# Second block's convolution: transforms ahead of products, filter layers two rounds apart, low parts on GpSimd

## What is computed

```python
def hyena_filter(length, fw1, fb1, fw2, fb2, fw3, fb3, fw4, freq):
    ...
    h = jnp.sin(freq * (emb @ fw1 + fb1))
    h = jnp.sin(freq * (h @ fw2 + fb2))
    h = jnp.sin(freq * (h @ fw3 + fb3))
    h = (h @ fw4).astype(jnp.float32)
    ...

def long_conv(u, filt):
    length = u.shape[1]
    uf = jnp.fft.rfft(u.astype(jnp.float32), n=2 * length, axis=1)
    kf = jnp.fft.rfft(filt, n=2 * length, axis=0)
    return jnp.fft.irfft(uf * kf[None], n=2 * length, axis=1)[:, :length]

def hyena_operator(u, conv_w, conv_b, filter_params, d_bias):
    uc = short_conv(u, conv_w, conv_b)
    x0, x1, v = jnp.split(uc, 3, axis=-1)
    z = v * x1
    filt = hyena_filter(u.shape[1], *filter_params)
    y = long_conv(z, filt).astype(z.dtype) + z * d_bias
    return y * x0
```

## Time and profile before

| | |
|---|---|
| runs | 3280.17 us median of 3 (3278.62 to 3293.43) |
| profiled execution | 3284.43 us, its span 3282.6 us |
| PE busy | 3092.4 us, 94% of the span |
| DVE, ACT, POOL busy | 50%, 38%, 8% |
| mean granted TensorE clock | 0.97 of full |
| chain that ended last | PE 82%, DVE 9%, ACT 4% |
| `even`, from the last attention rounds to the last inverse | 1780 to 1944 us from the span's start |

### The profile page before, as it was taken

One profiled execution on the slowest core, in us unless ns is written; L12 is line 12 of the kernel. 1 busy time (PEld: TensorE's weight loads), 2 busy tenths in 40 slices (PEclk: granted clock), 3 DMA queues, 4 the chain that ended last, 5 costly groups with the idle time before them and its releaser, 6 DMA issues.

```text
span 3282.6 us, 56668 instructions
## 1 busy us (share of the span) xinstructions
PE 3092.4 (94%) x24038; PEld 2843.1 (87%) x24038; DVE 1642.7 (50%) x2610; ACT 1232.1 (38%) x2089; POOL 255.1 (8%) x315
## 2 busy tenths in 40 slices
PE   6898989999898998999999889999999998999899
PEld 6787979977797997999977678999899998987899
DVE  5655565566555655333384455333443335335655
ACT  4454454434445444222244314212232223235443
POOL 1120010013101000000020110000100001101000
PEclk9999999999998998999999899999999998999999
DMA  4533555653365663333442113333433333343364
GB/s 163 184 119 112 178 194 182 215 169 112 108 198 168 202 228 109 123 103 96 149 133 63 58 57 127 115 121 102 131 117 109 119 115 130 126 149 102 121 195 141
DMA packets 266144, 446.72 MB, mean 136 GB/s; under 512 B 16723, under 2 KB 89316, under 8 KB 265252
## 3 DMA queue, kind: packets, MB, share of 16 engines
q1 hardware_dynamic: 260272, 430.80, 40.7%
q10 hardware_dynamic: 5620, 12.29, 1.1%
HBM read 441.98 MB, written 1.05 MB: 135 GB/s over the span
## 4 chain that ended last, share of the span: by engine, by line
PE 82%; DVE 9%; ACT 4%; issue 2%; DMA 1%; POOL 1%; ACTq 0%; SPq 0%; DVEq 0%; POOLq 0%
PE ps L1101 64%; PE ps L1305 2%; PE ps L1130 2%; DVE split L1815 2%; PE ps L1132 2%; PE ps L1131 2%; DVE AR L1815 2%; PE ps L1242 1%; ACT split L1524 1%; DVE A L1812 1%; DVE A L1867 1%; ACT A L1609 1%; PE ps L1253 1%; PE ps L1228 1%; DVE small L1979 1%
## 5 line engine op out<-in xcount | busy, mean ns | idle before, releaser
L1101 PEld LDWEIGHTS ps<-AR,split 128*128 128x128 f32 x19392 | 2265.0, 189 | 115.0 <-issue 77.5
L1101 PE MATMUL ps<-AR,split 128*128 128x256 f32 x19392 | 2330.7, 281 | 24.7 <-DVE AR L1815 10.6
L1815 DVE TENSOR_TENSOR split<-raw,split 128x1024 fp32r<-128x1024 f32 (+1 forms) x706 | 791.9, 1163 | 860.8 <-ACT split L1524 851.4
L1524 ACT ACTIVATE split<-raw 128x1024 fp32r<-128x1024 f32 (+1 forms) x728 | 682.3, 986 | 812.0 <-PE ps L1101 695.1
L1815 DVE TENSOR_TENSOR AR<-A,AR 128x256 fp32r<-128x256 f32 (+2 forms) x268 | 156.6, 585 | 28.2 <-ACT AR L1583 7.8
L2291 POOL TENSOR_TENSOR A<-A 128x256 f32<-128x256 f32 (+1 forms) x45 | 40.6, 902 | 1646.4 <-ACT A L1532 1483.3
L1812 DVE SCALAR_TENSOR_TENSOR A<-A,ps 128x256 f32<-128x256 f32 (+1 forms) x196 | 96.2, 506 | 125.5 <-ACT A L1567 121.1
L1571 ACT ACTIVATE AR<-A 128x256 fp32r<-128x256 f32 (+1 forms) x132 | 68.4, 525 | 191.6 <-DVE A L1901 191.4
L1567 ACT ACTIVATE A<-ps 128x256 f32<-128x256 f32 (+1 forms) x132 | 63.3, 490 | 151.1 <-PE ps L1101 150.9
L1901 DVE TENSOR_TENSOR A<-ps,A 128x256 f32<-128x256 f32 (+1 forms) x132 | 72.3, 555 | 90.2 <-PE ps L1101 90.0
L1130 PE MATMUL ps<-split,AR 128*128 128x512 f32 (+1 forms) x288 | 113.2, 393 | 0.0
(11 more groups left out here) (235 smaller groups left out, 2235.4 us busy)
## 6 DMA issues: line engine op xcount, KB each, us to landing
mod<-w_mod SPq DMA_DIRECT2D x288, 256.0 KB, 3.9
raw<-w_in SPq DMA_DIRECT2D x120, 512.0 KB, 4.8
raw<-w_gu SPq DMA_DIRECT2D x80, 512.0 KB, 4.7
raw<-ffn_a_in SPq DMA_DIRECT2D x80, 512.0 KB, 4.7
raw<-ffn_b_in SPq DMA_DIRECT2D x80, 512.0 KB, 4.6
raw<-ret_in SPq DMA_DIRECT2D x48, 512.0 KB, 4.6
raw<-w_down SPq DMA_DIRECT2D x44, 512.0 KB, 4.6
raw<-ffn_a_out SPq DMA_DIRECT2D x44, 512.0 KB, 4.7
```

Of the source, the lines that this page charges most:

```text
L1101: mm = e.matmul(out[:, s:s + NT], wt[:, c, m_], xs(k0 + c, a + s, a + s + NT), start=first and part + s == 0, stop=last and part == 2 and ...
L1524: e.activation(hi, self.raw_view(q), ACT.Copy).then_inc(*self.mark(("w hi", q)))
L1815: return self.e.tensor_tensor(out, v, hi.bitcast(F32), ALU.subtract)
```

## The change

Five things, all in `even`, `filter_chain` and `inverse`:

- `filter_layer` stands after two rounds of waiting in place of three. The first layer thus comes one round earlier, the second two, the third three.
- `modulation(i, 2)` moves from behind `hyena(0)` to ahead of it, right behind `hyena_z` and `load_dft`.
- `spectra(1, 0)` and `spectra(1, 1)` stand ahead of `products(0)`.
- After `fill(1)` come six chunks of `out`, then `inverse(0)`, then `products(1)`, ten more chunks, and `inverse(1)`.
- The low parts of the convolution's results move from DVE to GpSimd, and the ring `ct` has four buffers in place of two.

```diff
         self.load_dft()
+        self.modulation(i, 2)
         late = self.hyena_spectra()
...
-        ctb = self.ring("ct", 6144, 2, NT)
+        ctb = self.ring("ct", 6144, 4, NT)
...
-        self.modulation(i, 2)
         out = self.project_t("even out", self.io["even_out_2"][0], 0, 1024, both, self.add_mod(i, 5, 512, N), group=(0, 1, 2, 6, 3, 4), hurry=True)
-        self.products(0)
         for n in range(2):
             self.spectra(1, n)
+        self.products(0)
         self.fill(1)
+        for _ in range(6):
+            next(out)
+        self.inverse(0, cat2, ctb)
         self.products(1)
-        self.inverse(0, cat2, ctb)
-        for _ in range(16):
+        for _ in range(10):
             next(out)
         self.inverse(1, cat2, ctb)
         run(out)
...
-            for _ in range(3):
+            for _ in range(2):
                 yield
             self.filter_layer(n)
...
-            e.wait_ge(*self.after(("conv hi", s, m)))
-            self.low(cat2.lo(m, s * NT, (s + 1) * NT), cv, cat2.hi(m, s * NT, (s + 1) * NT)).then_inc(*self.mark(("cat2", m, s), ctb.freed(k)))
...
+    def inverse(self, s, cat2, ctb):
+        for m in range(4):
+            k, o = ctb.get()
+            hi, lo = (v(m, s * NT, (s + 1) * NT) for v in (cat2.hi, cat2.lo))
+            self.e.wait_ge(*self.after(("conv hi", s, m)))
+            self.e.tensor_tensor(lo, self.A[:, o:o + NT], hi.bitcast(F32), ALU.subtract).then_inc(*self.mark(("cat2", m, s), ctb.freed(k)))
```

## The result

The changed kernel takes 3277.93 us (median of 20 runs, 3269.33 to 3286.74). The kernel before, measured beside it, takes 3287.22 us (20 runs, 3276.82 to 3298.49). The ratio is 0.9962 with a 95% interval of 0.9951 to 0.9974, so the gain is 0.4%, 12.5 us of 3287 (8.5 to 16) by this ratio; the two medians lie 9.3 us apart. The forecast was a gain of 10.4 us, within 0.5%, and a median of 3270 us in a range of 3261 to 3278. The measured median lies 8 us above that one and just within the range. In a second comparison the changed kernel took 3274.77 us against 3287.10, ratio 0.9968 (0.9955 to 0.9981), again 10 to 12 us. The profiled execution of the changed kernel takes 3276.14 us, its span 3274.3 us, against 3284.43 and 3282.6 before.

A forecast was written before the change was run, and what follows sets the result against it. TensorE, busy 94% of the span, was taken as the bound, with time won only at its pauses and low clocks. 6.2 + 4.2 = 10.4 us off the median 3280.17 gave 3269.8, said as 3270 us, range 3261 to 3278.

The forecast's parts named there:

- The taps: At the taps, without the third filter layer there, DVE is free sooner and z starts 7.2 us earlier.
- The rounds: Attention rounds with three filter layers instead of two: taken as zero, ends 1.5 us of gain and 3.3 of loss.
- Rival 3: Attention rounds: each filter layer holds TensorE 5.1 us and leaves a low clock; slower, 3282.6 us; chance 0.05.
- The gains beside z: At z, gains and low parts stand until GpSimd finishes; transposes wait 2 to 3 us; cost 1.0 us (0 to 2.5).
- Part one in sum: Filter layers and gains moved to z, together: 7.2 + 0 - 1.0 = 6.2 us gained, ends 1.5 to 9.
- The fourth transform: In the second set it follows the third at once, saving 11.3 us; wait of 0.2 us ahead of the first inverse.
- The second inverse: Ahead of it a wait of 4.6 us (1.6 to 5) for products(1), then a low clock costing 1.9 us.
- part two: Transforms ahead of the products, through both inverses: 11.3 - 0.2 - 4.6 - 1.9 - 0.4 = 4.2 us gained, ends 3 and 10.
- (1): At z and the second inverse, no turns, clocks stay up: wait 1.6 us, gain 17.8, 3262 us; chance 0.15.
- (2): In both inverses GpSimd's low parts take 1.7 us each and bound them; gain falls by 5, 3275 us; chance 0.10.
- (4): Gain at the taps is waited for at z because DVE's sums end late: 1.5 us there, 3274.5 us; chance 0.08.

The follow-up runs named there:

- before again: The kernel before, unedited, second trace: taps start 41.91 us after the mark in the attention rounds, third residual update at 143.40.
- the run with DVE's low parts: Low parts of the convolution's results put back on DVE, against the changed kernel, ring still of four buffers: 3268.43 us.
- the gains late: `modulation(i, 2)` moved to just ahead of `inverse(1)`, against the changed kernel: 3264.90 us in a single execution.
- first pair: First traces of the kernel before and the changed kernel, no further edit: profiled executions of 3284.43 and 3276.14 us.
- the last version: Against the changed kernel: GpSimd's second-set crosses ahead of its low parts and after all first-set products, gains just ahead of `inverse(1)`: 3270.41 us, ratio 0.9945.
- the layers alone: Filter layers two rounds apart and nothing else, against the kernel before: 3281.35 us, the kernel before beside it 3283.72.
- second trace: The changed kernel traced again, unedited: third residual update 136.08 us after the mark in the attention rounds, 136.41 in its first trace.

## Why the prediction held, step by step

**The taps.** Forecast: z starts 7.2 us earlier by DVE's own work. Measured 7.26. The step from TensorE's pause of 5.39 us to DVE's end of the taps was the right one: TensorE's removed wait plus its shorter taps would have given more, and DVE's sums now hold it up by 1.13 us inside the taps. No part of the forecast named that wait. By itself it is covered, since z waits for DVE and not for TensorE, but a low clock stands behind it, which matters below.

**The rounds.** Forecast 0 (1.5 us of gain to 3.3 us of loss). What follows the last chunk of the rounds starts 39.09 us after the anchor before and at 39.36 in the changed kernel, with two low clock spells in each; at 35.89 and 36.91 in the two executions without one (before again, and the run with DVE's low parts). A loss of 0.3 to 1.0 us. The waits are 2.08 us for the scores (placed by hand: 1.6), 1.35 ahead of the second layer and 1.97 ahead of the transposes behind the third. All five table loads are there. Rival 3 (5.1 us a layer) falls.

**The gains beside z.** Forecast: a cost of 1.0, with a wait of 2 to 3 us ahead of the transposes and a low clock after it. The mechanism is there (4.67 us for two tiny instructions, low parts after z), the first copy is done some 10.3 us after z's start where 10.5 was forecast, and the cost is 0.5 to 0.6 us. But the wait ahead of the transposes is 0.27 us, not 2 to 3. The step that failed is the one that took TensorE's 48 matmuls ahead of z at full clock, 5.6 us. They take 7.39, because the granted clock is 0.50 from 1848 to 1851, two microseconds behind the new wait of 1.13 us in the taps. All nine traces with the layers two rounds apart have that wait (1.12 or 1.13 us) and a stretch at 0.50 that begins 1.2 to 2.4 us after it ends; the 48 matmuls take 6.8 to 8.4 us there. So the low clock came ahead of the wait for z and filled it, and did not follow it. What costs is the fourth transpose, as the forecast had it: z is 0.9 us shorter and the transposes start that much earlier against the taps than with the gains late, and the wait of 1.35 us for DVE's copy takes back more than that. Since this copy holds TensorE whatever it does ahead of it, the two wrong terms, the wait and the place of the low clock, cost the sum nothing.

**Part one in sum** was forecast at 6.2 us and measured at 6.6 (first pair). Between the two executions without a low clock spell in the rounds it is 5.8.

**The fourth transform.** The pause, the slow transform and the slow modulation, 11.3 us, are gone as forecast. The wait ahead of the first inverse was put at 0.2 and is 0.22 us.

**The second inverse.** The wait was put at 4.6 (1.6 to 5) and is 4.31 us. The forecast let eight products and four crosses take turns throughout, 10.7 us from the time DVE is free of the inverse; the rows show 10.3 (1911.50 to 1921.80), but otherwise divided: DVE makes two products at once, idles 3.21 us for the first pair of crosses, and takes turns with the second pair alone. So the size is right and the queue was in the forecast, but GpSimd's place in it weighs more and the turns less than the forecast had it. The low clock after it was put at 1.9 and costs 9.42 less 7.07, 2.35 us. The low part at the end was put at 0.4 and shows 0.27. GpSimd's low parts take 0.73 us, not 0.83, but the last, beside a product of DVE, 1.27. Not in the forecast: the sixty matmuls ahead of the stop take 7.42 us, and 60/96 of 11.25 are 7.03. The stop is not what makes them longer: they take 7.42 also with low parts on DVE, where none follows, and 7.17 in the last version, where 1.08 us follow. Why stays open. With some 0.15 us in the thirty-six ahead of the first inverse (4.37 for 4.22) that is the 0.5 us by which part two, measured at 3.6, stays under the sum (11.3 - 0.22 - 4.31 - 2.35 - 0.27 = 4.15; forecast 4.2). The Trainium skill, "SBUF — State Buffer", section "SBUF: two separate sides", says that a VectorE instruction with two SBUF inputs and a GpSimd instruction that reads SBUF lock each other out; DVE's 1.69 and 1.74 us for 0.68 agree.

**The rivals.** (1) needed both clocks up and no turns: 4.31 us of waiting with 0.50 behind it say no, though the last version shows that such a seam (43.75 us, 9 less than before) can be had by another order. (2) needed low parts of 1.7 us: they take 0.73. (4) falls by the layers alone. **The total**: forecast 10.4, the stage 10.2 in the first pair, 10.5 in the second trace, timed 12.5 (8.5 to 16) by the ratio and 9.3 by the medians. Nothing is given back later: the rest of the span takes 1330 to 1336 us in all traces, and the two kernels overlap in it. The forecast gain was right; the forecast median was not, since it started from 3280.17 us, a median of three, and the kernel before has 3287.22 in the larger set. That 3277.93 still lies in the range of 3261 to 3278, by less than 0.1 us, is luck.

## What to carry to other kernels

A wait on a shared engine's queue goes away only when the work ahead of it in that queue does. Moving a transform ahead of products, or chunks ahead of an inverse, carried the wait one step on, from 8.83 to 5.78 or 4.51 or 4.31 us; reordering the second engine's queue, so that the items someone waits for stand first and not beside the other engine's first products, took it to 1.08. Look at both queues of a pair that takes turns, and count a low clock of about 2 us behind each pause over 2 us that is left (1.5 to 2.7 us in these traces), and possibly one behind a shorter pause too. And compare one stage between two marks in common code, since the start alone moved by 16 us over all traces and by 9 on one chip.

## What the runs showed of the hardware

- Behind the same wait of 1.2 us the same matmuls ran once at about half the granted clock and once at full, in two executions of one kernel (3.62 and 2.02 us for sixteen). Behind waits of 2.26 to 4.5 us at the seam the clock was low every time: 2.26, 2.88, 4.31, 4.51 us of wait, 8.83, 8.59, 9.42, 9.82 us for an inverse of 7.07 to 7.14. Waits of 1.08 and 0.52 us at the seam had none. Yet a wait of 1.12 us inside the taps had a stretch at 0.50 behind it in nine traces of nine, which began 1.2 to 2.4 us after TensorE had taken up work again. So a low clock is to be looked for some microseconds behind a wait as well, and not in the next row alone.
- A GpSimd instruction of 128x256 took 0.73 us alone, 1.27 with a DVE product beside it; one of 128x512 1.27 us, one of 128x2048 4.60. Two DVE instructions of 128x8 took 4.67 us beside that last one, as long as it ran, and 0.24 us with GpSimd idle.
- What remains open: what decides, at a wait of 1 to 2 us, whether and when the clock falls. No run here tells it. The deeper ring was never run alone. The last version still leaves 1.08 us; low parts written behind DVE's products as well were not tried.
